# First mixer of a four-mixer transformer kernel: heads in pairs, placed beside the weight chunks

## The reference

```python
def even_mixer(h, w_in, cmp_pe, cmp_w1, cmp_w2, w_out, cos, sin):
    proj = jnp.einsum('btd,de->bte', h, w_in)
    qa, ka, va, qi, ki, wi, qb, kvb, gb = split_cols(proj, EVEN_SPLITS)
    ...
    o_a = dsa_attention(qa, ka, va, qi, ki, wi)
    ...
    o_b = nsa_attention(qb, k_c, v_c, k_s, v_s, k_w, v_w, gb, cmp_pe, cmp_w1, cmp_w2)
    o = jnp.concatenate([o_a.reshape(bsz, T, -1), o_b.reshape(bsz, T, -1)], axis=-1)
    return jnp.einsum('bte,ed->btd', o, w_out)
```

## Time and profile before

| | |
|---|---|
| Time, median of 3 runs | 1299.06 us (1297.97 to 1300.39) |
| Profiled execution, its own time | 1302.99 us |
| Its span in the profile | 1301.2 us |
| Mean granted TensorE clock | 0.942 |
| PE busy | 1218.7 us (94%) |
| DVE busy | 840.3 us (65%) |
| ACT busy | 584.9 us (45%) |
| Weights and other data moved | 248.96 MB, mean 191 GB/s |

### The profile page before, as it was taken

How to read it: one execution, slowest core, us unless ns; L and a number is a source line. 1 busy time by engine, 2 the same in 40 slices (tenths; PEclk the granted TensorE clock), 3 DMA queues, 4 the chain that set the end, 5 groups by cost and what they waited for, 6 DMA issues and landing times.

```text
span 1301.2 us, 18438 instructions
## 1 busy us (share of the span) xinstructions
PE 1218.7 (94%) x7598; PEld 1072.0 (82%) x7598; DVE 840.3 (65%) x1288; ACT 584.9 (45%) x881; POOL 44.6 (3%) x86
## 2 busy tenths in 40 slices
PE   4998988999999998989999957999999998999997
PEld 3994766899999886879999846999988987899996
DVE  5572545477777756768777765977775556755554
ACT  6201232464444646655444455444446544644442
POOL 1010000000000000000000000000001100000000
PEclk9898556999999999999999968999999999899999
DMA  7943110269776442358877503977764434355530
GB/s 283 199 142 119 44 65 33 94 261 354 282 278 252 147 145 98 130 213 328 316 284 279 216 31 139 355 290 286 289 226 162 130 130 178 120 205 194 194 129 33
DMA packets 35746, 248.96 MB, mean 191 GB/s; under 512 B 4272, under 2 KB 4288, under 8 KB 6608
## 3 DMA queue, kind: packets, MB, share of 16 engines
q1 hardware_dynamic: 26352, 189.13, 39.3%
q0 software_dynamic: 9168, 57.56, 13.1%
q10 hardware_dynamic: 144, 1.11, 0.2%
HBM read 243.06 MB, written 4.19 MB: 190 GB/s over the span
## 4 chain that ended last, share of the span: by engine, by line
PE 83%; DVE 10%; ACT 4%; issue 2%; DMA 1%; SPq 0%; DVEq 0%; ACTq 0%
PE bank L1196 68%; PE bank L1371 2%; DVE wlo L634 1%; PE bank L1557 1%; PE bank L1427 1%; PE bank L1385 1%; DMA raw<-in_stream 1%; DVE x L652 1%; DVE wlo L756 1%; DVE work L650 1%; PE bank L1274 1%; PE bank L1661 1%; DVE ul L679 1%; PE bank L1392 1%; ACT vo L382 1%
## 5 line engine op out<-in xcount | busy, mean ns | idle before, releaser
L634 DVE TENSOR_TENSOR wlo<-raw,whi 128x2048 fp32r<-128x2048 f32 x147 | 334.7, 2282 | 116.2 <-ACT whi L372 116.2
L1196 PE MATMUL bank<-uh,whi 128*128 128x256 f32 x1280 | 372.0, 291 | 2.9 <-DVE ul L679 2.9
L1196 PE MATMUL bank<-ul,whi 128*128 128x256 f32 x1280 | 363.9, 284 | 0.0
L1196 PE MATMUL bank<-uh,wlo 128*128 128x256 f32 x1280 | 363.7, 284 | 0.0
L372 ACT ACTIVATE whi<-raw 128x2048 fp32r<-128x2048 f32 x147 | 279.1, 1905 | 29.6 <-PE bank L1196 28.6
L1196 PEld LDWEIGHTS bank<-uh,whi 128*128 128x128 f32 x1280 | 247.3, 193 | 11.6 <-issue 9.5
L1196 PEld LDWEIGHTS bank<-ul,whi 128*128 128x128 f32 x1280 | 247.3, 193 | 5.0 <-issue 2.9
L1196 PEld LDWEIGHTS bank<-uh,wlo 128*128 128x128 f32 x1280 | 247.0, 193 | 0.0
L1196 PE MATMUL bank<-whi,hh 128*128 128x512 f32 x544 | 214.0, 393 | 0.0
L1196 PE MATMUL bank<-wlo,hh 128*128 128x512 f32 x544 | 212.4, 390 | 0.0
L1196 PE MATMUL bank<-whi,hl 128*128 128x512 f32 x544 | 211.8, 389 | 0.0
(11 more groups left out here) (235 smaller groups left out, 1282.1 us busy)
## 6 DMA issues: line engine op xcount, KB each, us to landing
raw<-in_stream SPq DMA_DIRECT2D x178, 1024.0 KB, 4.9
qk<-in_w_mod POOLq DMA_DIRECT2D x48, 1024.0 KB, 6.2
bias_rows<-PT POOLq DMA_DIRECT2D x1, 3072.0 KB, 36.2
u<-bias_rows POOLq DMA_DIRECT2D x16, 128.0 KB, 2.4
con<-in_con ACTq DMA_DIRECT2D x1, 1083.5 KB, 6.9
x<-in_x SPq DMA_DIRECT2D x2, 512.0 KB, 8.4
vo<-in_fin_g POOLq DMA_DIRECT2D x2, 512.0 KB, 5.3
out_y<-vo SPq DMA_DIRECT2D x2, 512.0 KB, 2.6
```

Source lines behind the costliest of these rows:

```text
L634: nc.vector.tensor_tensor(wlo[:, c % RING, 0:w], raw[:, raw_index(c) % RING, 0:w], whi[:, c % RING, 0:w].bitcast(fp32), ALU.subtract).then ...
L1196: ins = mm(out, st, mv, start=start and i == 0, stop=stop and i == 2, skip_group_check=True)
```

## The change

The first mixer is rebuilt like the other two attention mixers. Its twelve pairs of heads are laid beside the chunks, by tables of quarters. The whole of what changes:

- Chunks. Ten input chunks become eight with a split, two of them narrow (348 columns: all values, index weights and gates in one, for half of the input channels each), then chunk 2 (compressed keys and values), 3 (both key projections), 4 (queries), 5 (index queries), 6 (index key and key, one block), 7 (queries). Then the four compression chunks 8 to 11, then 12 and 13 (queries of the first attention), then the output chunks 14 to 17. These last four are now multiplied in float32 directly from `raw` (`even_back`), with no split on ACT and DVE.
- Heads. `pair_scores` computes two heads at once, one in rows 0 to 63 and one in rows 64 to 127. The masks are added by DVE in the same instruction that takes the maxima; the bf16 matmuls for them are gone. Of the two copies of turned probabilities in a pair, the first head's is ACT's and the second head's is DVE's.
- Rotary embedding. It is done in place in PSUM, the permuted part is accumulated on top by PE, and ACT makes the copy to `qk`.
- Outputs. `even_sums` scales and sums four heads, `even_out` turns them, and adds the part of the compressed blocks by matmul; ACT copies to `oT`.
- The start. PE begins with the norm of the first tile of tokens and the values of that tile, the second tile follows. The bias matmul stands after chunk 2. `act.wait_ge(bias_out, 16)` stands in ACT's program after the exponentials of `lam` and ahead of `hi_upto(4)` and of the copies of the values (`vt_ready`), for which chunk 3 waits on PE.

The tables, and the core of the three engines' programs:

```diff
+E_CC, E_KK, E_QB0, E_QI, E_KI, E_QB1, E_CMP, E_QA0, E_QA1, E_OUT = 2, 3, 4, 5, 6, 7, 8, 12, 13, 14
+
+E_ROPE = {E_CC: (KC, 2, False), E_KK: (KS, 0, False), E_QB0: (QB, 1, True), E_QI: (QI, 2, True), E_KI: (KA, 0, False),
+          E_QB1: (QB + 2, 2, True), E_QA0: (QA, 0, True), E_QA1: (QA + 2, 2, True)}
+E_ORDER = tuple(E_ROPE)
+E_SWAP = {(3, 1): 0, (4, 1): 1, (5, 1): 2, (6, 2): 3, (7, 1): 4, (8, 2): 5, (13, 1): 6, (14, 1): 7}
+E_INDEX = {(8, 0): 0, (8, 1): 1}
+E_SCORE = {(5, 3): 0, (7, 0): 1, (8, 2): 2, (9, 1): 3, (10, 1): 4, (11, 1): 5, (11, 3): 6, (12, 3): 7, (13, 2): 8,
+           (14, 1): 9, (14, 3): 10, (15, 2): 11}
+E_EXPS = {(5, 3): 0, (7, 1): 1, (8, 2): 2, (9, 2): 3, (10, 3): 4, (11, 1): 5, (12, 1): 6, (12, 3): 7, (13, 2): 8,
+          (14, 1): 9, (15, 0): 10, (15, 2): 11}
+E_TURN = {(6, 3): (0, 0), (7, 1): (0, 1), (7, 3): (1, 0), (8, 0): (1, 1), (9, 0): (2, 0), (9, 2): (2, 1), (10, 1): (3, 0),
+          (10, 3): (3, 1), (11, 0): (4, 0), (11, 1): (4, 1), (12, 0): (5, 0), (12, 1): (5, 1), (12, 2): (6, 0), (12, 3): (6, 1),
+          (13, 1): (7, 0), (13, 2): (7, 1), (14, 0): (8, 0), (14, 1): (8, 1), (14, 3): (9, 0), (15, 0): (9, 1),
+          (15, 2): (10, 0), (15, 3): (10, 1), (16, 0): (11, 0), (16, 1): (11, 1)}
+E_VALUE = {(7, 2): 0, (8, 1): 1, (9, 3): 2, (11, 0): 3, (11, 2): 4, (12, 2): 5, (13, 0): 6, (13, 3): 7, (14, 2): 8, (15, 1): 9,
+           (16, 0): 10, (16, 2): 11}
+E_TURN_OUT = {(13, 3): 0, (14, 1): 1, (15, 2): 2, (16, 3): 3}
+
+E_ROUND = ((8, 3), (9, 0), (9, 3), (10, 0), (10, 2), (11, 0), (11, 2), (12, 2))
+E_UNITS = tuple((i, u) for i in range(2, 18) for u in range(4))
```

ACT's start, its copies and its walk through the quarters:

```diff
-
...
+            act.wait_ge(bias_out, 16)
+
...
+            hi_upto(4)
+            for t in range(NT):
+                if t == 0:
+                    act.wait_ge(vt_ps, 1)
+                else:
+                    act.wait_ge(used, 2)
+                nc.scalar.activation(v_[:, t, 0:VT], bank[t][:, 0:VT], ACT.Copy).then_inc(vt_ready, 1)
+            act.wait_ge(vt_ready, NT)
+            nc.scalar.activation(gates[:, :, :], v_[:, :, VT_GATE:VT], ACT.Exp, scale=-1.0).then_inc(gate_exp, 1)
+            for i, q in E_UNITS:
+                if (i, q) in E_SWAP:
+                    r = E_SWAP[i, q]
+                    b0, k, _ = E_ROPE[E_ORDER[r]]
+                    act.wait_ge(e_sw, r + 1)
+                    b = bank[k][:, :].rearrange("p (b n) -> p b n", b=2)
+                    if b0 == KA:
+                        nc.scalar.activation(qk[0:64, KA, :], b[0:64, 0, :], ACT.Copy)
+                        nc.scalar.activation(qk[64:128, KI, :], b[64:128, 0, :], ACT.Copy).then_inc(e_add, 1)
+                    else:
+                        nc.scalar.activation(qk[:, b0:b0 + 2, :], b, ACT.Copy).then_inc(e_add, 1)
+                if (i, q) in E_INDEX:
...
+                if (i, q) in E_TURN and E_TURN[i, q][1] == 0:
+                    p, c = E_TURN[i, q]
+                    act.wait_ge(s_tr["e"], 2 * p + c + 1)
+                    if p >= 1:
+                        act.wait_ge(s_pv["e"], p)
+                    nc.scalar.activation(PT[:, c, :], bank[5][:, 0:384], ACT.Copy).then_inc(s_pt["e"], 1)
```

PE's program (the waits of `pair_scores` and `pair_values`, the start, the compression and the output chunks):

```diff
             def pair_scores(ph, p):
-                pe.wait_ge(d_add if ph == "d" else b_copied, 2 * (p // 2) + 2)
+                if ph == "e":
+                    qb, kb, _ = even_map(p)
+                    pe.wait_ge(e_add, 3 if p < 4 else 6 if p < 8 else 7 if p < 10 else 8)
+                    if p == 2:
+                        pe.wait_ge(e_ir, 4)
+                else:
+                    qb, kb = p, 8 + p
+                    pe.wait_ge(d_add if ph == "d" else b_copied, 2 * (p // 2) + 2)
                 if p:
...
+            def even_values():
+
+                for t in range(NT):
+                    for g in range(2):
+                        if t == 0:
+                            pe.wait_ge(lo_ready, g + 1)
+                        wh, wl = [p[:, g, 0:4 * VT].rearrange("p (k n) -> p k n", k=4) for p in (whi, wlo)]
+                        for k in range(4):
+                            pe.wait_ge(ul_ready, ul_no(0, t) + 2 * g + k // 2 + 1)
+                            ts = slice(128 * t, 128 * t + 128)
+                            ins = three(bank[t][:, 0:VT], False, wh[:, k, :], wl[:, k, :], uh[:, 4 * g + k, ts],
+                                        ul[:, 4 * g + k, ts], g == 0 and k == 0, g == 1 and k == 3)
+                        if t == 1:
+                            ins.then_inc(used, 1)
+                        elif g == 1:
+                            ins.then_inc(vt_ps, 1)
+                        if t == 0 and g == 0:
+                            norm(0, 1)
+
...
+            def compress(i, steps):
+
+                kv, half = (i - E_CMP) // 2, (i - E_CMP) % 2
+                n = PLAIN_CMP + i - E_CMP
                 pe.wait_ge(loaded[n % RING], loaded_value(n))
                 w1 = raw[:, n % RING, :].rearrange("p (k n) -> p k n", k=KB)
                 for k in range(KB):
-                    ins = mm(bank[7][0:30, 256 * kv:256 * kv + 256], blk[:, kv, KB * half + k, :], w1[:, k, :],
-                             start=half == 0 and k == 0, stop=half == 1 and k == KB - 1)
+                    if k % 2 == 0:
+                        steps(k // 2)
...
+            def even_back(c, steps):
+
+                n = PLAIN_OUT + c
+                pe.wait_ge(loaded[n % RING], loaded_value(n))
+                pe.wait_ge(e_oc, c + 1)
+                w = raw[:, n % RING, :].rearrange("p (k n) -> p k n", k=2)
                 for t in range(NT):
-                    for h in range(8):
-                        g = h // 4
-                        rr = slice(64 * g, 64 * g + 64)
-                        c = 128 + 4 * NBLK * t + NBLK * (h % 4)
-                        ins = mm(bank[6 + g][:, c:c + NBLK],
-                                 qk[rr, QB + h % 4, 128 * t:128 * t + 128], kcm[rr, NBLK * g:NBLK * g + NBLK],
-                                 start=True, stop=True)
-                ins.then_inc(sc_ps, 1)
-
-            pe.wait_ge(e_add, 9)
-            pe.wait_ge(e_sel, 1)
-            for i in range(24 + 3):
-                if i < 24:
-                    q, r0, k, vv, vs, ob = even_map(i)
-                    scores("e", i, q, k, r0, causal + chosen if i < 8 else causal)
-                if i < 4:
-                    hidden(i // 2, i % 2)
-                if i == 5:
...
+                ins.then_inc(plain_used, 1)
+
+            pe.wait_ge(in_con, 16)
+            norm(0, 0)
+            even_values()
+            for i in range(2, 14):
+                steps = even_steps(i)
+                if E_CMP <= i < E_CMP + 4:
+                    if i == E_CMP:
+                        pe.wait_ge(blk_ready, 1)
+                        pe.wait_ge(bias_sb, 1)
+                    elif i == E_CMP + 2:
+                        pe.wait_ge(e_add, 3)
+                    compress(i, steps)
+                    continue
+                m = split_index(i)
+                pe.wait_ge(lo_ready, m + 1)
+
+                if i in (E_KK, E_QB0):
+                    pe.wait_ge(vt_ready, i - E_KK + 1)
+                elif i > E_QB0:
+                    pe.wait_ge(e_add, {E_QI: 1, E_KI: 2, E_QB1: 4, E_QA0: 5, E_QA1: 6}[i])
+                features(m, bank[E_ROPE[i][1]], blocks=1 if i == E_KI else 2, steps=steps).then_inc(used, 1)
+                if i == E_CC:
+                    pe.wait_ge(in_misc, 64)
+                    mm(bank[6][0:16, 0:384], relb, hot, start=True, stop=True).then_inc(bias_T, 1)
+            for c in range(4):
+                even_back(c, even_steps(E_OUT + c))
+            norm(1, 0)
+            mlp(0, True)
```

More of the change, by code:

```diff
@@ L526, in hi_beside @@
                     hi_half(m0 + i + 3, q // 2)
-            out_upper(0, one)
-            hi_upto(MLP0 + 1)
             for t in range(NT):
@@ new lines, in _ @@
+            for i, q in E_UNITS:
+                if q == 0 and i - 1 in E_ROPE:
+                    r = E_ORDER.index(i - 1)
+                    b0, k, scaled_ = E_ROPE[i - 1]
+                    dve.wait_ge(used, split_index(i - 1) + 1)
+                    if r >= 2:
+                        dve.wait_ge(e_sw, r - 1)
+                    rope_in_place(bank[k], scaled_, r, 1 if b0 in (KC, KA) else 2).then_inc(e_t2, 1)
+                if (i, q) in E_VALUE and E_VALUE[i, q] % 2:
+                    even_sums(E_VALUE[i, q] // 2)
+                if (i, q) == (5, 3):
+                    blocks_of_keys()
+                elif (i, q) == (10, 0):
+                    gelu_in(0, bank[6][0:30, 0:256])
+                elif (i, q) == (10, 2):
+                    gelu(0, bank[6][0:30, 0:256])
+                elif (i, q) == (11, 0):
+                    hidden_keys()
+                elif (i, q) == (11, 2):
@@ L1430, in pair_scores, with index_pair @@
                             ins.then_inc(s_ps[ph], 1)
+            def index_pair(a):
+                pe.wait_ge(ki_in, 32)
```

(16 more changed lines are left out.)

759 lines of the change are left out of this document (335 added, 424 removed).

## The result

The changed kernel takes 1268.62 us (median of 4 runs, 1266.48 to 1270.44); the kernel before took 1299.72 in the same session (1297.97 to 1303.47). The ratio is 0.9756 with a 95% interval of 0.973 to 0.9783: 31 us faster, where 44 had been forecast. The time lies inside the forecast's range of 1244 to 1275 us, 13.6 us above the 1255 that was forecast. The profiled execution took 1270.44 us, the longest of the four; its span, from the first to the last instruction, is 1268.6.

The account below looks back on a forecast made before the run. It took the first mixer's head loop as bound by PE at 1.2 GHz. Terms 71.9 + 127.5 + 6 + 2 + 0.7 + 8.1 = 216.2 us against 259.94, 43.7 less: 1255 us, range 1244 to 1275.

Parts of the forecast that it names:

- The bound: First mixer's head loop: PE runs small matmuls at 1.2 GHz, granted clock 0.52, busy 79 of 85 us.
- The wait: After chunk 2, PE idles 35 us for the 3 MB bias-row write, taken as 32 us, until 71.9.
- short write: Rival, 6%: the wait for the bias rows is 9 us instead of 32, giving 1232 us.
- From there to the last matmul of the projection: First mixer after the wait: 127.5 us of PE work, 6 of stalls, 2 of clock.
- Stalls: PE's waits beside the first mixer's chunks: 6 us, bounds 0 and 20.
- late pairs: Rival, 17%: PE waits at many quarters for pairs' maxima, exponentials and copies; 1267 us, or 1285 if wholly uncovered.
- The clock: After the 35 us wait PE restarts at a lower clock, costing 2 us, then the clock stays up.
- slower by the clock: Rival, 4%: the clock falls in the compression chunks and stays down until the MLP; 85 us more, 1340.
- the reason that was given against it: In the first mixer, whole chunks with a split lie between small matmuls; the other two mixers never stayed down.
- PE's work: First mixer from the wait to the projection's end: matmuls at full clock sum to 127.5 us.
- Into the MLP: Tile 0's norm starts 0.7 us after the last projection matmul; 8.1 us from it to the MLP's third group.
- Behind the mixer: From the MLP's third group of matmuls on, the program is as before, with its parts taking the same time.

Follow-up runs that it names:

- e7: Kernel before, with ten extra unused 128-column matmuls in each of ten heads of the first mixer's loop; 1324.39 us (one run).
- e9: Kernel before, with 24 extra unused 128-column matmuls in each of ten heads of the first mixer's loop; 1354.88 us.
- e11: Kernel before, with 12 extra unused 512-column matmuls in each of ten heads of the first mixer's loop; 1310.8 us.
- e5_copies_by_act: Changed kernel, with both copies of turned probabilities of each pair made by ACT; 1266.78 us (one run).
- e2_own_rows: Changed kernel, with the bias rows in a tile of their own, so ACT's wait for their write falls; 1253.51 us (one run).
- e13_rows_in_pieces: Changed kernel, bias rows in their own tile, key-gathering DMAs issued earlier, the 3 MB write sent in 16 pieces during the second MLP; 1233.55 us.
- e3: Changed kernel, bias rows in their own tile and eight small compressed-key DMAs ahead of the 3 MB write on POOL's queue; 1242.75 us.
- e8: Changed kernel, bias rows in their own tile, the eight compressed-key DMAs and two index-key copies ahead of the 3 MB write; 1244.22 us.
- e10: Changed kernel, bias rows in their own tile, all ten small DMAs first, the 3 MB write held until the first output chunk is done; 1245.76 us.

## Why the prediction was right, and where its sizes were off

**The bound** was read rightly: e7, e9 and e11 show that PE at half clock set the head loop, and in after the same pieces have the lengths of the third mixer.

**The wait** was the largest single term. Forecast: bias matmul done at 36.8, landing at 69.4, PE on at 71.9. Measured: issue at 37.47, 33.79 us for the write in place of 32 (inside the bounds of 30.0 and 36.2), landing at 71.26, PE on at 73.68: 1.8 us late. The rate alone was 101 GB/s after 105 in the earlier trace rows, with 0.97 of the engines' time. The rival "short write" is refuted by that. By the Trainium skill, "DMA: Bandwidth & Descriptors", section "Anatomy of one DMA — SWDGE (gpsimd) path", the write would be an estimate of 9.2 us; this case's traces show 33.8 to 36.8 in every kernel that wrote it whole.

**From there to the last matmul of the projection** the forecast had 127.5 of work, 6 of stalls and 2 of clock, from 71.9 to 207.4. PE's last such matmul ended at 215.5, 8.1 late, of which 1.8 is the wait above.

- Stalls were smaller than forecast. From 73.7 on, PE is idle for some 0.6 us to 80, 0.1 to 90 and 3.2 to 210, together 3.9 in place of 6. Of the 3.2, 1.5 lie from 150 to 160 us, where DVE is busy for 9.33 of 10 us with a lower part, the sums of the outputs and the softmax over the blocks; the rest lies near 122 and 136 us. The rival "late pairs" didn't come.
- The clock cost about 4 and not 2: it stood at 0.59 for the 9.8 us of PE work between 73 and 84 us, and at 1.00 from there on. The rival "slower by the clock" didn't come, and e11_before_wide, where wide matmuls between the small ones bring the clock back, fits the reason that was given against it.
- PE's work was the term that was mis-sized: 8.1 - 1.8 - 2 + 2.1 leaves 6.4 us, so it was about 134 and not 127.5. I added up PE's matmuls in the trace from start to start, without its idle time. The input chunks take 44.1 us, some 40 without the clock's 4, after a forecast of 37.4. The twelve pairs take 35.3 after 33.6; a turning beside the compression chunks is 0.48 and not 0.33. The sixteen quarters of compression chunks take 15.5 after 14.3 (0.98 each, or 1.84 for two in a row, where a fourth of 3.57 is 0.89). The small matmuls of the compression path take 3.4 after 2.6. The output chunks (27.9 after 27.5), the index scores and the turned outputs had their forecast lengths. Up to the start of the matmul behind them, the eight rotary permutations take 5.6 after 6.0. In the chain, whose pieces go from end to end and after a wait from start to end, they take 7.8: three full ones for which PE had just waited are 1.12 or 1.13 and not 0.86, one without a wait is 1.05, and two are 0.86. Much of the excess thus lies where PE goes from one kind of work to another or starts again after a wait. Why such a seam costs what it does, no run shows. The chain, a stretch with both a permutation after a wait and a pair's scores:

```profile
100.74 1.13 PE bank L1520 x2
101.87 0.71 PE bank L1218 x6
102.58 0.33 PE bank L1425 x3
102.91 0.71 PE bank L1218 x6
103.62 0.86 PE bank L1400 x8
104.47 1.63 PE bank L1218 x12
```

Twelve matmuls of a chunk take 1.42 us with only a turning between them, but 1.63 behind a pair's scores.

**Into the MLP.** 8.1 us were forecast from the norm of tile 0 to the third group; it is 8.03 (215.85 to 223.88). So the MLP's third group stands at 223.9 in place of 216.2, and the gain up to there is 36.1 in place of 43.7.

**Behind the mixer** I had said that the program is as before and so costs the same. In the profiled execution it took 3.4 us more (1268.6 - 223.9 = 1044.7 after 1301.2 - 259.9 = 1041.3). That isn't a cost of the change: in e5_copies_by_act, whose program behind the mixer is the same as after's, the stretch took 1040.8 us, and 1041.9 in e2_own_rows. It is within what executions differ by behind this point. Part of it can be seen. The norm ahead of the fourth mixer ran at another clock; the first line is after, the second the same work in before, 35 us later:

```profile
945.00:955.00 10.00, 8.16 (x33) 6.52 (x32) 7.11 (x18) 7.72 (x15) 1.76 (x4) 0.83 0.04 13
```

```profile
980.00:990.00 10.00, 8.16 (x40) 6.43 (x39) 7.07 (x19) 7.08 (x15) 1.11 (x3) 1.00 0.01 2
```

PE is equally busy, but the clock is granted at 0.83 in one and 1.00 in the other. Between the turnings of the third and of the fourth MLP, the lead of after shrinks from 35.6 to 33.6 us. The last 1 us of the 3.4 I can't place, and I had no row that could foretell in which execution an unchanged stage meets a dip of the clock.

**What the range and the rivals lacked.** The forecast was 1255.4 before rounding, 13.2 us too low: 7.7 at the MLP's third group, 3.4 behind it, and 2.1 because the profiled execution of after lies 1.8 us above its median where before's lay 3.9 above. The range held, but partly by luck: its upper end was made of 14 us more of stalls, and the stalls came out smaller than forecast; the write's length, the clock, PE's own work and the spread between executions, which had no room of their own beyond 4 us for the write, added to less than that. None of the rivals said that the wait, priced rightly, could simply be avoided. By the medians e13_rows_in_pieces is 65.9 us below before (1299.45 in its session), and after is 31.1 below; so the added wait and the write's place took back 35. How much of the 65.9 is the rebuild's alone stays open, since before carried the write as well, beside its own loads, and the kernel before without it wasn't run.

## What to carry to other kernels

A wait added for the safety of a shared tile is priced by all that stands behind it; here a tile of 1.5 KB in each of 16 partitions gave back 14 us, and 28 with eight small DMAs moved ahead of the transfer. When such a wait goes, ask what the transfer itself holds back, on its queue and beside it. Here it cost nothing once it was sent in pieces at a place where its readers were far and PE had work in hand; which of the two did it wasn't tested. And in a sum made of whole chunks' rates, small work laid between their quarters needs a term of its own for the seams, here 6 us in 134.

## What the runs showed of the hardware that I had not expected

- One slow DMA starves the others. The 3 MB write with 1.5 KB rows moved 100 to 105 GB/s where nothing or little else was under way, but took 0.96 to 0.99 of the engines' time. Beside it a 1 MB weight load landed in 21.3 and 22.0 us, where the pages' median is 4.8 or 4.9; behind it on the same queue the 64 KB copies `qk<-qk` took 11.2 us in place of 1.9, and the gathers `u<-qk` 33.4 in place of about 5. In one piece, with no engine waiting for its end as such, it still cost 10 to 13 us at the mark in three places (e3, e8 and e10 against e13_rows_in_pieces), and 24.6 with the gathers behind it on the queue (e2); sixteen pieces of 192 KB at the late place cost nothing that the trace shows.
- A PE that is busy for 20 of 20 us can stay at 1.2 GHz: it did with 24 matmuls of 128 columns added to each head (granted clock 0.50 in e9_before_filler24), and with twelve of 512 columns in their place it rose to 2.4 GHz (1.00, e11_before_wide). The small ones cost 0.213 us each at the lower level, the wide ones 0.234 at the upper.
